# An encoder block on one core: the PEER gate matrix built by 384 indirect DMAs that add, in place of one-hot products

## The reference, cut to what matters

```python
def peer_ffn(h, w_q, sub_keys, expert_u, expert_v):
    q = (xt @ w_q).reshape(T, PEER_HEADS, 2, PEER_HALF)
    s = jnp.einsum('thpc,pnc->thpn', q, sub_keys)
    top_s, top_i = lax.top_k(s, PEER_TOPK)                  # 16 of 128, per half
    cand_s = top_s[:, :, 0, :, None] + top_s[:, :, 1, None, :]
    best_s, best_pos = lax.top_k(cand_s.reshape(T, PEER_HEADS, kk), PEER_TOPK)
    ...
    gate = jax.nn.softmax(best_s, axis=-1)
    # per token: 8 heads x 16 experts
    a = jnp.einsum('tkd,td->tk', expert_u[idx], xs)
    hid = jax.nn.gelu(a, approximate=False) * g
    return jnp.einsum('tk,tkd->td', hid, expert_v[idx])
```

## Time and profile before

| | |
|---|---|
| median of three executions | 4517.12 us |
| the profiled execution's own time | 4515.92 us |
| its span, first to last instruction | 4514.1 us |
| PE busy, share of the span | 98% |
| POOL busy, share of the span | 50% |
| score stage, DMA share in 3010 to 3400 us | 0.36 |
| last stage, DMA share in 3620 to 4090 us | 0.94 |

### The profile page before, as it was taken

One profiled execution on the slowest core, in us unless ns is written; L12 is line 12 of the kernel. 1 busy time (PEld: TensorE's weight loads), 2 busy tenths in 40 slices (PEclk: granted clock), 3 DMA queues, 4 the chain that ended last, 5 costly groups with the idle time before them and its releaser, 6 DMA issues.

```text
span 4514.1 us, 60832 instructions
## 1 busy us (share of the span) xinstructions
PE 4415.1 (98%) x21733; PEld 3839.1 (85%) x21733; DVE 2031.7 (45%) x3430; ACT 1382.8 (31%) x1811; POOL 2273.8 (50%) x1100
## 2 busy tenths in 40 slices
PE   6999999999999999999999999999999999999998
PEld 6877788888887877888888888888889999999998
DVE  6222443234435433994003566620003377767765
ACT  5222333333334433222222222222223332333332
POOL 5332244443443444444444444444446888889774
PEclk9999999999999999999999999999999999999999
DMA  6554366655667873233333444453335699999983
GB/s 232 179 172 128 114 195 191 191 185 186 189 199 231 265 224 112 88 105 121 119 120 135 146 167 146 160 200 118 122 121 179 217 327 343 330 331 348 350 311 108
DMA packets 523290, 869.44 MB, mean 193 GB/s; under 512 B 30272, under 2 KB 358336, under 8 KB 504640
## 3 DMA queue, kind: packets, MB, share of 16 engines
q1 hardware_dynamic: 384896, 566.30, 38.4%
q10 hardware_dynamic: 115776, 167.69, 10.7%
q0 software_dynamic: 22528, 134.30, 7.9%
HBM read 784.55 MB, written 217.84 MB: 222 GB/s over the span
## 4 chain that ended last, share of the span: by engine, by line
PE 77%; POOL 5%; DMA 2%; DVE 2%; issue 1%; ACT 1%; ACTq 0%; DVEq 0%
PE banks L1697 25%; PE banks L1698 25%; PE banks L1699 24%; POOL w_lo L610 4%; DMA arena<-expert_rows_scratch,constants 2%; POOL constants L592 1%; PE banks L2013 1%; PE banks L1870 1%; POOL arena L602 1%; DVE arena L1621 0%; ACT w_hi L624 0%; PE banks L1961 0%; DVE arena L1165 0%; DVE x_lo L1627 0%; PE banks L1904 0%
## 5 line engine op out<-in xcount | busy, mean ns | idle before, releaser
L1697 PE MATMUL banks<-x_hi,w_hi 128*128 128x512 f32 (+1 forms) x6464 | 2421.5, 375 | 29.1 <-DVE x_lo L1627 9.3
L1698 PE MATMUL banks<-x_lo,w_hi 128*128 128x512 f32 (+2 forms) x6592 | 2444.9, 371 | 0.0
L1699 PE MATMUL banks<-x_hi,w_lo 128*128 128x512 f32 (+1 forms) x6464 | 2406.5, 372 | 0.0
L570 POOL TENSOR_TENSOR w_lo<-w_raw,w_hi 128x1024 fp32r<-128x1024 f32 x572 | 1387.7, 2428 | 1994.0 <-ACT w_hi L624 1994.0
L1697 PEld LDWEIGHTS banks<-x_hi,w_hi 128*128 128x128 f32 x6464 | 1216.2, 188 | 210.2 <-issue 16.9
L1698 PEld LDWEIGHTS banks<-x_lo,w_hi 128*128 128x128 f32 x6592 | 1242.5, 188 | 166.0 <-issue 1.4
L1699 PEld LDWEIGHTS banks<-x_hi,w_lo 128*128 128x128 f32 x6464 | 1215.2, 188 | 174.4
L624 ACT ACTIVATE w_hi<-w_raw 128x1024 fp32r<-128x1024 f32 x824 | 865.9, 1057 | 1501.5 <-PE banks L1699 1403.6
L610 POOL TENSOR_TENSOR w_lo<-w_raw,w_hi 128x1024 fp32r<-128x1024 f32 x252 | 607.6, 2420 | 140.8 <-ACT w_hi L624 137.2
L1652 DVE SCALAR_TENSOR_TENSOR banks<-arena,constants,banks 128x2048 f32<-128x2048 f32 x127 | 298.8, 2352 | 156.5 <-DMA arena<-expert_rows_scratch,constants 155.4
L1627 DVE TENSOR_TENSOR x_lo<-arena,x_hi 128x384 fp32r<-128x384 f32 x128 | 118.8, 928 | 409.2 <-ACT x_hi L1025 409.0
(11 more groups left out here) (231 smaller groups left out, 2429.4 us busy)
## 6 DMA issues: line engine op xcount, KB each, us to landing
expert_rows_scratch<-w_v SPq DMA_DIRECT2D x256, 512.0 KB, 5.1
w_raw<-w_u SPq DMA_DIRECT2D x256, 512.0 KB
w_raw<-w_v SPq DMA_DIRECT2D x256, 512.0 KB
w_raw<-w_in SPq DMA_DIRECT2D x200, 512.0 KB
gate_matrix_scratch<-arena ACTq DMA_DIRECT2D x12, 2048.0 KB, 7.3
early_mix_or_one_hots<-gate_matrix_scratch ACTq DMA_DIRECT2D x32, 768.0 KB
constants<-gelu_scratch ACTq DMA_DIRECT2D x128, 192.0 KB
gelu_scratch<-arena ACTq DMA_DIRECT2D x86, 256.0 KB, 2.0
```

Source lines behind the costliest of these rows:

```text
L570: nc.gpsimd.tensor_tensor(wlo[s][:], raw[s][:], whi[s][:], ALU.subtract).then_inc(w_lo_made, 1)
L1697: M.matmul(out, whi[s][:, k], h, start=f, stop=False)
L1698: M.matmul(out, whi[s][:, k], l, start=False, stop=False)
L1699: ins = M.matmul(out, wlo[s][:, k], h, start=False, stop=e)
```

## The change

The gate matrix is laid out as [128, 128, 384]: j, i, token, 25 MB in all. It is first set to zero: DVE fills a tile (early_b) with zeros, and SP stores it 16 times, 1.5 MB each, behind the halves 24 to 39 of w_in. ACT waits for these stores before it loads early_b with other data. Later DVE works out, for each of the 384 tokens and each of its 128 picks, the place of the gate in that layout (16 index steps in place of 8). Then POOL issues 384 indirect DMAs (3 tiles of 128 tokens by 128 picks), each of which adds one gate per token, 128 values of 4 bytes, into the matrix in memory. They stand behind the w_lo of the halves from chunk 32 of the score stage on, two, two and three in turn, in the order head, tile of tokens, pick. Before the first of the 16 picks of a head and tile POOL waits until all earlier ones of that tile have landed. ACT waits for all of them after chunk 115, and loads the first gates, gelu values and the residual from there on. The nine transposes, the one-hots, the 384 matmuls of line 2013, the reductions and the twelve stores are gone. The last stage loads the gates of four j in runs of 384 tokens (1536 bytes), where it had runs of 32 tokens by four j (512 bytes).

```diff
@@ sizes
-U_1, U_2, U_3, U_B, U_C = 24, 8, 8, 48, 40
-TB = 32
+U_1, U_2, U_C = 24, 92, 12
 TD = T - P
-NTB = TD // TB
+TG = TD // P
+SCATTER_FROM = 32
+N_INDEX = 16
+def scatters_at():
+    order = [(tt, TOPK * h + k) for h in range(PH) for tt in range(TG) for k in range(TOPK)]
+    return {h: order[7 * h // 3:7 * (h + 1) // 3] for h in range(-(-3 * len(order) // 7))}
...
-        gmat_dram = dram("gate_matrix_scratch", [NTB, P, NK, TB])
+        gates_dram = dram("gate_matrix_scratch", [NK, P, TD])
@@ SP, in stream_and_move
+                    if w is w_in and n in range(24, 40):
+                        sp.wait_ge(zeros_made, 1)
+                        sp.dma_start(gates_dram[HT * (n - 24):HT * (n - 23)].rearrange("j p t -> p j t"), zeros)\
+                            .then_inc(gates_zeroed, 16)
@@ POOL
-            low_halves(2 * C_PQ + 4, 2 * C_V + 4)
+            low_halves(2 * C_PQ + 4, 2 * (C_U + SCATTER_FROM))
+            gate_values = gates_dram.rearrange("j i (t o) -> (j i t) o", o=1)
+            def add_gate(tt, e):
+                if tt == 0 and e == 0:
+                    pool.wait_ge(sparse_index, N_INDEX)
+                    pool.wait_ge(gates_zeroed, 16 * NK // HT)
+                if e % TOPK == 0 and e:
+                    pool.wait_ge(gates_added[tt], 16 * e)
+                nc.gpsimd.indirect_dma_start(gate_values, bass.IndirectOffsetOnAxis(gate_index[:, tt, e:e + 1], 0),
+                                             sel[:, 2, tt, e:e + 1], None, compute_op=ALU.add)\
+                    .then_inc(gates_added[tt], 16)
+            for m in range(2 * (C_U + SCATTER_FROM), 2 * C_V + 4):
+                pool.wait_ge(w_hi_made, m + 1)
+                nc.gpsimd.tensor_tensor(wlo[m % 4][:], raw[m % 4][:], whi[m % 4][:], ALU.subtract)\
+                    .then_inc(w_lo_made, 1)
+                for tt, e in SCATTERS.get(m - 2 * (C_U + SCATTER_FROM), []):
+                    add_gate(tt, e)
@@ ACT
+            act.wait_ge(gates_zeroed, 16 * NK // HT)
             act.dma_start(early_a[:], mix_dram[0:2].rearrange("k p t -> p k t")).then_inc(mix_in[0], 16)
...
             expert_chunks(U_1, U_2)
-            expert_chunks(U_1 + U_2, U_3)
-            act.wait_ge(sel_saved, 2)
-            first = U_1 + U_2 + U_3
-            with act.Fori(0, NTB // 2) as i:
...
-                        act.dma_start(gmat_dram[2 * i + b], gstage[:, b]).then_inc(gmat_out[b], 16)
+            for t in range(TG):
+                act.wait_ge(gates_added[t], 16 * P)
             def load_gates(s, r):
-                act.dma_start(gsb[:, r], gmat_dram[:, :, bass.ds(8 * s + 4 * r, 4), :]
-                              .rearrange("b p j t -> p b (j t)")).then_inc(gmat_in[r], 16)
+                act.dma_start(gsb[:, r], gates_dram[bass.ds(8 * s + 4 * r, 4)].rearrange("j p t -> p j t"))\
+                    .then_inc(gates_read[r], 16)
...
-            expert_chunks(first + U_B, U_C - 2, early_a)
+            expert_chunks(U_1 + U_2, U_C - 2, early_a)
@@ DVE
+            V.memset(early_b[:], 0.0).then_inc(zeros_made, 1)
...
-            dve.wait_ge(sel_turned, 3)
-            V.tensor_copy(ghi[:, 0:TD], bank[6][:, 0:TD]).then_inc(sel_saved, 1)
...
+            index_step(6, V.scalar_tensor_tensor(gate_place, sel[:, 1, 0:TG], float(P), sel[:, 0, 0:TG],
                                                  ALU.mult, ALU.add))
+            for t in range(TG):
+                index_step(7 + t, V.tensor_scalar(gate_place[:, t], gate_place[:, t], float(TD), small[:, 68 + t:69 + t],
+                                                  ALU.mult, ALU.add))
+            index_step(10, V.tensor_copy(gate_index, gate_place))
...
-            with dve.Fori(0, NTB // 2) as i:
...
-                    V.tensor_tensor(oh_j[:, slots, 0], at_j, of_four(early_a[:, 0], i, q), ALU.mult)
...
-                save_gates(15)
             def product(s, k):
-                dve.wait_ge(gmat_in[k // 4], 16 * s + 16)
+                dve.wait_ge(gates_read[k // 4], 16 * s + 16)
...
+                V.tensor_tensor(htmp[:, k % 2], agb[:, k % 4], gsb[:, k // 4, k % 4], ALU.mult).then_inc(hid_product, 1)
@@ PE
-            expert_chunks(2, U_1 - 2)
-            expert_chunks(U_1, U_2)
-            pe.wait_ge(gate_soft, 3)
-            for k in range(3):
-                for tt in range(TT - 1):
-                    ins = M.transpose(bank[4 + k][:, P * tt:P * tt + P], sel[:, k, tt], ident)
...
-            with pe_loop(0, NTB // 2) as i:
...
-                        for k in range(4):
-                            slot = 4 * (q % 2) + k
-                            ins = M.matmul(bank[2 + k // 2][:, 2 * P * (k % 2):2 * P * (k % 2) + 2 * P], oh_i[:, slot],
-                                           oh_j[:, slot].rearrange("p h j -> p (h j)"), start=True, stop=True)
...
-            expert_chunks(first + U_B, U_C)
+            expert_chunks(2, NK - 2)
```

More of the change, by code:

```diff
@@ L78 @@
 ROW_LAG = 3
-assert U_1 + U_2 + U_3 + U_B + U_C == NK and U_B == 8 * (NTB // 2)
+SCATTER_FROM = 32
+N_INDEX = 16
+assert U_1 + U_2 + U_C == NK
 assert N_MEM_GATES + DIL_S * N_DIL_GATES + HG * N_HG_GATES == N_GATE
@@ L330, in encoder_block_kernel @@
         gate_soft = sem("gate_soft")
[L331 to L337, removed]
+        zeros_made = sem("zeros_made")
+        gates_zeroed = sem("gate_matrix_zeroed")
+        gates_added = [sem(f"gates_added{t}") for t in range(TG)]
         gelu_out = [sem(f"gelu_out{b}") for b in range(2)]
         residual_in = sem("residual_in")
-        gmat_in = [sem(f"gmat_in{b}") for b in range(2)]
+        gates_read = [sem(f"gate_matrix_in{b}") for b in range(2)]
         gelu_in = [sem(f"gelu_in{b}") for b in range(4)]
@@ L536, in stream @@
                         sp.dma_start(raw[s][:], w[4 * i + s]).then_inc(w_loaded[s], 16)
+            zeros = early_b[:].rearrange("p a b -> p (a b)").rearrange("p (j t) -> p j t", j=HT)
             row_pieces = v_rows.rearrange("(jb jl i) (kt d) -> jb kt i jl d", jl=HT, i=P, d=P)
@@ L588, in gather_act @@
                 if e == 0:
-                    pool.wait_ge(sparse_index, 8)
+                    pool.wait_ge(sparse_index, N_INDEX)
                     for b in range(2):
@@ L644, in _ @@
             act.sem_inc(acc2_free, 2)
-            for s_ in (*gate_out, dil_out, hg_out, *gelu_out, *gmat_out):
+            for s_ in (*gate_out, dil_out, hg_out, *gelu_out):
                 act.sem_inc(s_, 16)
@@ new lines, in _ @@
+            for t in range(TG):
+                index_step(7 + t, V.tensor_scalar(gate_place[:, t], gate_place[:, t], float(TD), small[:, 68 + t:69 + t],
+                                                  ALU.mult, ALU.add))
+            index_step(10, V.tensor_copy(gate_index, gate_place))
+            index_step(11, V.tensor_scalar(small[:, 78:79], small[:, 79:80], float(TD), None, ALU.add))
+            index_step(12, V.scalar_tensor_tensor(hid_sparse, sel[:, 1, TT - 1], float(P), sel[:, 0, TT - 1],
+                                                  ALU.mult, ALU.add))
@@ L1615, in product @@
+            index_step(13, V.tensor_copy(v_index, hid_sparse))
+            index_step(14, V.tensor_scalar(act_sparse, hid_sparse, float(T), small[:, 78:79], ALU.mult, ALU.add))
+            index_step(15, V.tensor_copy(act_index, act_sparse))
+            index_step(16, V.tensor_copy(gate_sparse, sel[:, 2, TT - 1]))
             def product(s, k):
-                dve.wait_ge(gmat_in[k // 4], 16 * s + 16)
+                dve.wait_ge(gates_read[k // 4], 16 * s + 16)
                 dve.wait_ge(gelu_in[k % 4], 32 * s + 16 * (k // 4 + 1))
```

76 lines of the change are left out of this document (9 added, 67 removed).

## The result

The kernel with the change takes 4642.9 us, the median of four executions (4638.01 to 4646.81). Beside it on the same chip the kernel before took 4517.23 us (four, 4507.05 to 4517.95). The ratio is 1.0285, with a 95% interval of 1.0273 to 1.0298: slower by 126 us. The forecast was 4464, the range ended at 4612, and R1, the rival with a dearer add, stood at 4611. The profiled execution took 4638.01 us, its span 4636.2, the mean granted clock 0.989.

What follows compares the result with a forecast made beforehand. TensorE's stream of products, busy 98% of the span, was taken as the bound. From 4515.9 us, -48.4, -0.9 and -4 gave 4462.6, forecast as 4464 us by the runs' median; the range was 4450 to 4612.

Steps and rivals of the forecast that it cites:

- R1: Score stage, slower rival: the add's three accesses against two make a scatter 1.44 us on POOL, +147 us, 4611; 27%.
- part 2: Score stage: POOL's 384 indirect DMAs at 0.96 us each make 5.21 us a half, hidden below PE's 5.44.
- upper end of 1.34: Score stage: dearest price of one scatter on POOL, from the gathers, giving 6.10 us a half.
- +110 and +147: Score stage: POOL's excess over 5.44 us by 165 halves, at 1.34 and at 1.44 us a scatter.
- R2: Score stage, rival: a scatter costs POOL 1.10 us as in the busy stretch, +17 us, 4481; 14%.
- Part 1: Gate-building stretch: PE's one-hot products and nine transposes go, saving 48.4 and 0.90 us, -49.3 together.
- The index steps and their waits: Before the scatters: index steps end by 2267, POOL reaches chunk 32 at about 2301; hidden, 0 us.
- R4: Score stage, slower rival: scatters land serially at 3 us each, POOL waits at each group of 16; +254, 4718; 5%.
- Part 3: Zeroing between 215 and 298 us: DVE's memset and SP's 16 stores delay weights within their cover; 0 us.
- R3: Early weights, rival: the zero stores stall PE by 10 us, 4474; 6%.
- The cover ahead of ACT: Zeroing: slack between a weight's landing and ACT's rounding; with w_lo ready 12.8 us early, 28 us of cover in all.
- Part 4: Last stage: longer gate runs win back between 0 and 9.8 us of stalls; half of 8 taken, -4.

Runs made afterwards that it cites:

- e2: The changed kernel with all 384 scatters as plain writes, without the add; 4463.87 us, ratio 0.9892.
- e1: The changed kernel with its 384 scatters and ACT's wait for them left out; 4461.23 us, ratio 0.9887.
- e4: The changed kernel with all 384 adding scatters, but w_lo of score-stage halves 64 to 231 made by DVE, not POOL; 4459.87 us, ratio 0.9881.
- e9: The changed kernel with all 384 adding scatters, each of 64 rows and not 128; 4587.23 us, ratio 1.017.
- e6: e4 with each of the 16 zero stores followed by a second 1.5 MB store to another scratch tensor; 4521.78 us, ratio 1.0012.
- e5: e4 with the last stage's gates loaded in runs of 512 bytes again; 4458.06 us, ratio 0.9866.
- e3: The changed kernel with every second scatter left out, 192 at 7/6 per half; 4459.86 us, ratio 0.9883.

## Why the prediction was wrong, by its steps

**What failed: part 2's choice of 0.96 us for an adding DMA.** It was taken from plain gathers, and its upper end of 1.34 too. e2 measures the plain scatter at 0.973 and its time at 4463.9; the instruction that adds takes 1.557. The rest of the step stands. Its formula, 2.97 + 2.33 d, gives 6.60 us at d = 1.557, and the timeline has 6.63. The excess is (6.63 - 5.44) x 165 = 196 us, less POOL's lead of three halves on PE (16 us), which the prediction's +110 and +147 left out: 180. The trace has the same: in 2300 to 3390 the count of one matmul in three is 1603 in e1 and 1339 in the kernel after, 264 x 0.6794 = 179 us. The bound of 1.34 was drawn from rows that hold no add, though the text said that no row shows one. A bound for an unseen variant has to be wider than the scatter of the seen one.

**R2, and why 0.96 held for the plain form.** The prediction chose 0.96 over 1.10 by the DMA share. That was the right value for a reason that the traces don't bear out; and what sets the two prices, which R2 had in no row, the timelines of DVE and POOL show together. In the kernel before, all 72 gathers of line 592 that start while DVE runs line 1621 or 1627 (two tiles in, one out) take 1.09 us or more, and of the 56 others all but one take 0.95 or 0.96, in the quiet stretch and in the busy one. They take longer by what DVE's instruction has left, less 0.13 us, and so do e4's scatters. Lines 1652 and 1671, which read or write banks, do no such thing. In the score stage of the kernel after DVE idles, so 0.96 was to be expected of a plain scatter whatever the DMA share.

**R1 had the right place and sign, but not the mechanism.** It scaled the price by three accesses to two, 1.44 us. The measured factor is 1.60, and e9 shows that what POOL pays hardly follows the rows (2.3 ns a row of some 1.56 us), so a count of accesses per element cannot be the whole of it. What POOL does in the add's 0.58 us, and how much of that is fixed, no run here shows. The packets do multiply, 148 in place of 32 per scatter; the Trainium skill's rule of two read descriptors per chunk ("Collectives: The Full Stack", The bandwidth ceiling) points the right way for the traffic, and the trace shows more than a doubling there. e4, which keeps all of this traffic and loses nothing, shows that it costs no time. R1's 27% looks too small: only an argument about 8 KB rows, and no row with an add, spoke against it. The result is 32 us beyond its 4611.

**Part 1, -49.3 us: right.** PE's halves are 5.44 us in e1 over the stretch where they were 5.94.

**The index steps and their waits, 0: right.** The first scatter starts at 2304.1, as soon as its turn comes (forecast 2301), and POOL waits for no group of 16 (its only idle time before line 599 is 0.3 us or less each), which also ends R4. In e4 a scatter lands in 3.1 us (median, 5.3 at most).

**Part 3, zeros, 0: right.** w_lo at 380.30 in the kernel after stands at 379.19 before, so 1.1 us. R3 falls. The queue fell back more slowly than forecast: SP issues a weight every 6.84 us (245.27 to 313.67, ten halves), where 7.8 was forecast, so 22 us after sixteen and not 38. The cover ahead of ACT (15 of the 28) was used up, and w_lo came late by up to 4.5 us (310.73 against 306.21), inside the 12.8 us that it is ready early. Beyond the whole cover the delay does reach PE, as e6 shows.

**Part 4, -4: within its bounds, about half of what e1 has, not shown in cause.** 3620 to 4090 has 904 of the line, in the 890 to 905 that were named, though the stretch is another part of the stage by now; the like one has 903. e1 recovers 15 matmuls of the 800 us, 7.8 us, against the kernel before. Over all eight executions with long runs it is 3 to 19, 1.6 to 9.9 us, against a single execution of the kernel before. How much of it the runs' length brings is not settled (e5). The DMA share does fall. The Trainium skill's 512 B as the run from which line rate holds ("DMA: Bandwidth & Descriptors", Specifications) gives zero, and no time here contradicts it; the queue's own share (14.6 against 13.3%) does differ above 512 B.

**The sum.** 4515.9 - 49.3 - 7.8 + 1.1 = 4459.9, and e1, e3 and e4 have 4461.2, 4459.9 and 4459.9. Add 179: 4639, and the profiled execution has 4638.0. No term of more than a few microseconds is missing. Closer than that it can't be read: executions of one kernel differ by up to 11 us, and e1 to e4 stand beside a kernel before of 4513.07.

## What to carry to other kernels

Ask of an in-order engine how full it will be, not whether the new work costs something: 96% full with an unmeasured price in it is a coin toss, and the loss of an overfull engine is paid for every half. When an operation is a variant that the trace does not show, an add on a DMA here, don't price it by its plain form; a single measured instruction of that form would have given the price. And when a change frees an engine, look at what stands on the overfull one and can move there: here DVE's w_lo turned +2.8% into -1.2%.

## What was not expected of the hardware

- An indirect DMA that adds takes 1.557 us on POOL against 0.973 without the add, 1.407 with 64 rows, and 1.54 to 1.80 (median 1.685) when it gathers.
- The w_lo behind it starts 1.00 us after its start and runs beside it, and takes 2.97 us in place of 2.40, so that nothing is won.
- An adding scatter of 128 values of 4 B makes 148 packets and 0.39 us of all 16 DMA engines; without the add 32 packets and 0.02 us.
- An indirect DMA that starts on POOL while DVE works on two tiles neither of which is in banks takes longer by what DVE has left, less 0.13 us: 2.40 and not 1.55 us in e4 with 0.99 us left, 1.10 and not 0.96 in the kernel before with 0.27.
- ACT loads its tables more often in the kernel after (144 loads against 60, of them 59 at line 649 and 47 at line 1008, 1283 ns each), with no time lost on the path, as e1 has the same 144.
